# Adding halves of a group's squares on VectorE before the product of ones, and a new order in the norms

## The chip, the cores and the metric

The kernel runs on one core of one Trainium2 chip. The time is device microseconds of one execution. Most executions of this kernel agree within a few tenths of a microsecond.

## What is computed

The reference runs 512 tokens of width 1024 (with 16 meta tokens ahead in the first part) through a stack of layers in f32: differential and forgetting attention with an MLP, retention with an MLP, then a block that merges sparse attention with a state-space scan (SSD), and a last gated feed-forward. Two parts of it matter here.

Layer norm, four times (behind each mixer and each MLP), and RMS norm at other places:

```
mu = mean(x);  var = mean(square(x - mu));  y = (x - mu) * rsqrt(var + eps) * g + b
```

The gated group norm behind the scan, once for each of four groups of 512 channels:

```
u = y * silu(z);  u = u * rsqrt(mean(u * u, over the group's 512 channels) + EPS)
```

## The kernel before

Activations lie by feature: `x32` holds 8 tiles of 128 features x 528 columns (16 meta columns and 512 tokens), so a mean over features is a sum over partitions and tiles. The kernel makes it on TensorE with a stationary matrix of equal values (`ones_d`, `ones_g`). Such a product of f32 data is two matmul records of 512 columns; the 16 meta columns, in the wide norms, are two short ones more. The dense products split weights and activations in a high and a low part (f32r) and take three products for each pair.

**Weights** come through a ring of four slots (RING, AHEAD = 3). SP loads a chunk of 128x1024, ScalarE makes `w_hi` (L362), VectorE `w_lo` (L370), both three chunks ahead of the chunk that TensorE reads. SP loads a slot again when `lo_ready` says that VectorE is done with it.

Each engine has one hand-written program, and all order between engines is by semaphores. An engine that waits holds up all that stands behind in its program.

**The scan stage** (`ssm_pe`, `ssm_act`, `ssm_dve`) goes through four groups g of four chunks c each, then a fifth turn, g = 4, that only finishes the last group. Between the scan's own small products TensorE runs "items", dense chunks of other projections (`xs`, `z`, `so`, `gate`), 24 products each. The finish of group g-1 lies in the first chunk of group g:

- VectorE, at the end of group g-1, multiplies the gate in (L3161, four of 128x512), then makes group g's first chunk ready (`chunk_ready`, L3065 to L3094: dec_end, eight of seg, x_dt, b_tok, cb, x_dec, seg, c_dec), then the first item's w_lo, then `finish_norm_dve` (L3125), which waits for the root.
- ScalarE squares the four tiles into `z_buf` (L2975, `u_sq` + 1 each), does its part of chunk_ready, one w_hi, loads the logarithm's table (L1167), takes the logarithm of the mean (L1173, waits for `ssm_var`) and the exponential (L1176), which makes the inverse root.
- TensorE runs `ssm_turn`, the first item, then `squares_pe` (L2891), four products of `ones_g` with the four tiles of `z_buf`, then the next items and `ssm_outputs`.
- `so_pe` (L2876) of the group, some chunks later, multiplies the normed tiles. In the last group POOL loads `merged` back once `u_lo` is written.

**LayerNorm** (L1249) is spread over the product ahead of it. `tile_dve` (L1306) adds tile k's product to x32, sums tiles 5 and 6 into `rest` (the sum of tiles 0 to 4 made a shift, which is taken off all tiles into `xc`), and adds squares into `sq_sum` (`squares_sum`, L1334), those of tile 6 ahead of tile 7. ScalarE squares (`squares_act`). `LayerNorm.pe` (L1293) then runs filler products (`idle_products`, 18 for ln00, 12 for ln10, none for the others) and four sums: rest, sq_sum, tile 7 of x32 (the mean is whole) and the square of tile 7 (the variance is whole), and more fillers. ScalarE copies the mean (L1406), squares it (L1409), loads the logarithm's table (L1167) and makes the root of what VectorE writes at L1381 (variance less squared mean).

The callers are `even_out_dve` (L1004) for ln00 and `before_norm_dve` (L1126) for ln01, ln10 and ln11: for each chunk of the product ahead they split w_lo and call `tile_dve`. ln00 has nl = 0 and ln10 has nl = 2.

**Norm** (L1178) with `summed=True` is the RMS norm of `rms_ffn` and of `final`, the last work of the kernel: the squares of tiles 0 to 6 are summed by VectorE into `x_sum`, that of tile 7 comes from ScalarE. `final` runs ten fillers first.

Of the kernel before, what the change touches and what calls it, by code (L numbers as in the profile page):

```python
# [7 lines left out]
ALU = mybir.AluOpType  # L8
# [6 lines left out]
KT = D // P  # L15
META = 16
SEQ = 512
# [22 lines left out]
AHEAD = RING - 1  # L40
# [12 lines left out]
CHUNKS = dict(STAGES)  # L53
# [149 lines left out]
def program(nc, x_in, weights, params, tables, lam_in, w_uk, w_uv, rel, line, skewed, cum_dram, acum_dram, merged_dram, kept_dram, gate_dram, sums_dram, out):  # L203
    with ExitStack() as ctx:
# [799 lines left out]
        def even_out_dve(dve):  # L1004

            halves_before = halves_signalled(len(dense_step) - 1)
            for ck in range(4):
                split_lo(dve, Step(FIRST_CHUNK["eo_b"] + ck + AHEAD))
                for m in range(2):
                    ready = (chunk_done, FIRST_CHUNK["eo_b"] + ck + 1) if m else (half_done, halves_before + ck + 1)  # L1010
                    ln00.tile_dve(dve, "eo_b", 2 * ck + m, 1.0, ready)

        MEANS = {26: 0, 27: 1, 30: 2, 31: 3, 32: 4}

# [111 lines left out]
        def before_norm_dve(dve, name, factor, norm, outs=(), split_before=0):  # L1126

            kg = KGROUPS.get(name, 1)
            for c in range(CHUNKS[name]):
                if c >= split_before:  # L1130
                    split_lo(dve, Step(FIRST_CHUNK[name] + c + AHEAD))
                if c % kg == kg - 1:
                    norm.tile_dve(dve, name, c // kg, factor, (chunk_done, FIRST_CHUNK[name] + c + 1),
                                  out=outs[c // kg] if c // kg < len(outs) else None)

        def before_norm_act(act, name, norm, split_before=0):

# [40 lines left out]
        class Norm:  # L1178
# [28 lines left out]

            def pe(self, pe):
                if self.summed:
                    if self.last:  # L1210
                        idle_products(pe, 10, 6)
                    pe.wait_ge(sum_added, self.sums + KT - 1)
                    nc.tensor.matmul(flat[:, 3072:3072 + SEQ], ones_d[:], x_sum[:, META:T], start=True, stop=False, skip_group_check=True)
                for n, k in enumerate(self.squares):
                    pe.wait_ge(norm_squared, self.squares_before + n + 1)
                    last = nc.tensor.matmul(flat[:, 3072:3072 + SEQ], ones_d[:], self.sq[:, k, META:T],
                                            start=k == 0, stop=k == KT - 1, skip_group_check=self.summed)
                last.then_inc(norm_var, 1)
                if not self.last:
                    idle_products(pe, 22)  # L1220
# [28 lines left out]
        class LayerNorm:  # L1249
# [4 lines left out]
            def __init__(self, name, tile, wide, g, b, last=False):  # L1254
                self.sums = norms["sums"]
                norms["sums"] += KT - 2
                self.last = last
                split = norms["split"]
                norms["split"] += not last
                self.tile, self.wide, self.g, self.b = tile, wide, g, b  # L1260
                self.c0 = 0 if wide else META
                placed["next"] = norm_start
                self.xc = at(name + "_xc", [P, KT, T])
                self.sq = at(name + "_sq", [P, 3, T])
                self.sq_sum = at(name + "_sq_sum", [P, T])
                self.shift = at(name + "_shift", [P, T])
                self.rest = at(name + "_rest", [P, T])
                self.mean = at(name + "_mean", [P, T])
                self.mean_sq = at(name + "_mean_sq", [P, T])
                self.rt = at(name + "_rt", [P, T])  # L1270
                self.n, self.nl = norms["all"], norms["layer"]
                norms["all"] += 1
                norms["layer"] += 1
                self.hi_before = KT * split
                self.ready = (norm_lo, KT * split)
                self.lo_at = KT * (split + 1)
# [16 lines left out]
            def pe(self, pe):  # L1293
                idle_products(pe, {0: 18, 2: 12}.get(self.nl, 0), 6)
                pe.wait_ge(sum_added, self.sums + KT - 2)
                pe.wait_ge(ln_copied, 3 * self.nl + 1)
                self.sums_pe(2048, ones_d, self.rest, True, False)
                pe.wait_ge(ln_summed, self.summed_before() + KT - 2)
                self.sums_pe(3072, ones_d, self.sq_sum, True, False)
                tiles_out(pe, self.tile)  # L1300
                self.sums_pe(2048, ones_d, x32[:, KT - 1], False, True).then_inc(ln_means, 1)
                pe.wait_ge(ln_squared, KT * (self.nl + 1))
                self.sums_pe(3072, ones_d, self.sq[:, (KT - 1) % 3], False, True).then_inc(norm_var, 1)
                idle_products(pe, 27 if self.wide else 26)

            def tile_dve(self, dve, name, k, factor, ready, out=None):  # L1306
                u = FIRST_TILE[name] + k
                if k > SHIFT_TILES:
                    self.squares_sum(dve, {5: range(2, 4), 6: range(4, 6), 7: range(6, 7)}[k])
                dve.wait_ge(*ready)  # L1310
                o = halves(x32[:, k], self.wide)
# [18 lines left out]
                    nc.vector.tensor_tensor(self.xc[:, j, c], x32[:, j, c], self.shift[:, c], ALU.subtract).then_inc(ln_less, 1)  # L1330
                if k == SHIFT_TILES:
                    self.squares_sum(dve, range(1, 2))

            def squares_sum(self, dve, tiles):  # L1334
                c = slice(self.c0, T)
# [1550 lines left out]

        def squares_pe(pe, g):

            for t in range(4):
                pe.wait_ge(u_sq, 4 * g + t + 1)  # L2890
                last = nc.tensor.matmul(bank(1, SEQ), ones_g[:], z_buf[:, t], start=t == 0, stop=t == 3)  # L2891
            last.then_inc(ssm_var, 1)

        def ssm_pe(pe, g):
# [232 lines left out]
        def finish_lo_dve(dve, g):  # L3127
            x = xs[g % 2]
            for t in range(4):
                dve.wait_ge(u_hi_s, 4 * g + t + 1)  # L3130
                nc.vector.tensor_tensor(u_lo[:, t, META:T], x[:, t], u_hi[:, t, META:T], ALU.subtract).then_inc(u_lo_s, 1)

        waiting = []

        def ssm_dve(dve, g):

            for c, items in enumerate(group_items(g)):
                if g < SSM_GROUPS:
                    chunk_ready(dve, g, c)
                for item in waiting:  # L3140
                    item_dve(dve, item)
                waiting.clear()
                for i, item in enumerate(items):
                    item_split(dve, item, split_lo)
                    if g and c == 0 and i == 0:
                        finish_norm_dve(dve, g - 1)
                    if g and c == 0 and i == (0 if item[0] == "z" else 1):
                        finish_lo_dve(dve, g - 1)
                        item_dve(dve, items[0])
                    if not (g and c == 0 and i == 0):  # L3150
                        if item[0] == "xs" and i == len(items) - 1:
                            waiting.append(item)
                        else:
                            item_dve(dve, item)
                if g < SSM_GROUPS:
                    chunk_end(dve, g, c)
# [603 lines left out]
```

## Time and profile before

| | |
|---|---|
| median of 3 runs | 2673.89 us (2673.74 to 2673.92) |
| the profiled execution | 2673.44 us |
| its span, first to last instruction | 2671.6 us |
| TensorE matmul / weight load busy | 98% / 84% of the span |
| VectorE, ScalarE, GpSimd busy | 63%, 47%, 7% |
| mean granted TensorE clock | 0.998 |
| HBM read, written | 438 MB, 160 MB |
| chain that ended last | TensorE 85%, VectorE 8%, ScalarE 4%, issue 2%, DMA 1% |

Busy shares say which engine works, not which one is waited for. In the timelines a row is a run of instructions: start, length, engine, line, operation, tiles, count, and in brackets how long the engine was idle before it and what ended that. Rows of pipelined matmuls overlap by about 0.17 us, so a run of 512-column f32 records takes 0.43 us for each, and the last one 0.59. The windows give busy time of each engine in a stretch, the granted clock (PEclk, 1.00 is 2.4 GHz) and the DMA share.

### The profile page before, as it was taken

The page shows a single profiled execution, that of the slowest core. Times are in us where ns is not written, and L with a number is a line of the kernel's source. Part 1 is how long each engine was busy: PE and PEld are TensorE (multiplying, and loading weights), DVE is VectorE, ACT ScalarE, POOL GpSimd, SP SyncE. Part 2 cuts the span into 40 slices and gives each one's busy share as a digit, 9 for nine tenths or more (in the row PEclk, how much of TensorE's full clock was granted, in tenths as well). Part 3 has the DMA queues.
Part 4 walks back from the last instruction along what each step waited for, and adds up shares of the span by engine and source line. Part 5 has one row for each costly group of instructions (what it writes and reads, how often), then busy time and mean ns, then how long its engine had stood idle before and what let it go on. Part 6 is the DMA issues. An engine that isn't in the chain of part 4 may idle for free.

```text
span 2671.6 us, 42472 instructions
## 1 busy us (share of the span) xinstructions
PE 2617.3 (98%) x16495; PEld 2237.1 (84%) x16495; DVE 1675.3 (63%) x2902; ACT 1267.8 (47%) x2049; POOL 183.2 (7%) x234
## 2 busy tenths in 40 slices
PE   8999999999999999999999999999999999999998
PEld 7877789999998798779898786766877777799996
DVE  4544586265565465487265535875589986696784
ACT  4556465153364354356154434254464554475561
POOL 1111000000000000000000012051000000000000
PEclk9999999999999999999999999999999999999999
DMA  9994836958646564736557979922433333254451
GB/s 357 219 229 104 218 88 224 218 167 245 142 159 216 145 188 138 236 105 192 148 163 246 260 182 266 256 58 79 144 95 119 113 112 115 79 189 148 156 171 55
DMA packets 187722, 450.56 MB, mean 169 GB/s; under 512 B 14984, under 2 KB 31368, under 8 KB 186896
## 3 DMA queue, kind: packets, MB, share of 16 engines
q1 hardware_dynamic: 108368, 264.29, 29.3%
q0 software_dynamic: 60000, 167.78, 26.6%
q10 hardware_dynamic: 19168, 15.93, 2.1%
q8 instruction: 127, 2.08, 0.3%
q14 instruction: 59, 0.48, 0.1%
HBM read 438.24 MB, written 159.51 MB: 224 GB/s over the span
## 4 chain that ended last, share of the span: by engine, by line
PE 85%; DVE 8%; ACT 4%; issue 2%; DMA 1%; POOL 0%; DVEq 0%; ACTq 0%; POOLq 0%
PE ps L399 30%; PE ps L1531 25%; PE ps L549 6%; PE ps L3328 4%; PE ps L2339 2%; PE ps L1976 2%; PE ps L2130 2%; PE ps L2014 2%; PE ps L2876 2%; PE ps L791 2%; PE ps L919 1%; DVE w_lo L370 1%; ACT w_hi L362 1%; PE ps L878 1%; DVE xs L3029 1%
## 5 line engine op out<-in xcount | busy, mean ns | idle before, releaser
L370 DVE TENSOR_TENSOR w_lo<-raw,w_hi 128x1024 fp32r<-128x1024 f32 x500 | 611.0, 1222 | 472.7 <-ACT w_hi L362 471.6
L362 ACT ACTIVATE w_hi<-raw 128x1024 fp32r<-128x1024 f32 x500 | 527.0, 1055 | 517.5 <-PE ps L399 296.5
L1531 PE MATMUL ps<-x_hi,w_hi 128*128 128x264 f32 (+1 forms) x1120 | 317.4, 283 | 2.2 <-DVE rg L1910 0.7
L1531 PE MATMUL ps<-x_hi,w_lo 128*128 128x264 f32 (+1 forms) x1120 | 316.4, 282 | 0.0
L1531 PE MATMUL ps<-x_lo,w_hi 128*128 128x264 f32 (+1 forms) x1120 | 316.1, 282 | 0.0
L399 PE MATMUL ps<-x_hi,w_hi 128*128 128x512 f32 (+1 forms) x688 | 249.4, 380 | 16.1 <-DVE w_lo L370 9.4
L399 PE MATMUL ps<-x_lo,w_hi 128*128 128x512 f32 (+1 forms) x688 | 245.2, 374 | 0.0
L399 PE MATMUL ps<-x_hi,w_lo 128*128 128x512 f32 (+1 forms) x688 | 244.0, 372 | 0.0
L1531 PEld LDWEIGHTS ps<-x_hi,w_hi 128*128 128x128 f32 x1120 | 210.8, 188 | 5.1 <-issue 2.2
L1531 PEld LDWEIGHTS ps<-x_hi,w_lo 128*128 128x128 f32 x1120 | 211.1, 188 | 0.0
L1531 PEld LDWEIGHTS ps<-x_lo,w_hi 128*128 128x128 f32 x1120 | 210.6, 188 | 0.4
L399 PE MATMUL ps<-h_hi,w_hi 128*128 128x264 f32 (+1 forms) x768 | 205.8, 322 | 0.0
L399 PE MATMUL ps<-h_lo,w_hi 128*128 128x264 f32 (+1 forms) x768 | 205.2, 322 | 0.0
L399 PE MATMUL ps<-h_hi,w_lo 128*128 128x264 f32 (+1 forms) x768 | 204.6, 320 | 0.0
L399 PEld LDWEIGHTS ps<-x_hi,w_hi 128*128 128x128 f32 x688 | 125.5, 189 | 50.9 <-issue 18.7
L399 PEld LDWEIGHTS ps<-x_hi,w_lo 128*128 128x128 f32 x688 | 125.5, 190 | 23.3
L399 PEld LDWEIGHTS ps<-x_lo,w_hi 128*128 128x128 f32 x688 | 125.4, 189 | 22.9 <-issue 1.0
L399 PEld LDWEIGHTS ps<-h_lo,w_hi 128*128 128x128 f32 x768 | 127.7, 188 | 11.6 <-issue 0.2
L399 PEld LDWEIGHTS ps<-h_hi,w_lo 128*128 128x128 f32 x768 | 127.8, 189 | 11.2
L399 PEld LDWEIGHTS ps<-h_hi,w_hi 128*128 128x128 f32 x768 | 127.1, 188 | 11.6 <-issue 0.2
L549 PE MATMUL ps<-x_hi,w_hi 128*128 128x264 f32 x352 | 112.6, 320 | 0.0
L549 PE MATMUL ps<-x_hi,w_lo 128*128 128x264 f32 x352 | 100.4, 285 | 0.0
(501 smaller groups left out, 5823.9 us busy)
## 6 DMA issues: line engine op xcount, KB each, us to landing
raw<-in_weights SPq DMA_DIRECT2D x255, 512.0 KB
raw<-weight_sums SPq DMA_DIRECT2D x280, 256.0 KB
weight_sums<-in_weights POOLq DMA_DIRECT2D x36, 1536.0 KB, 20.2
raw<-in_weights SPq DMA_DIRECT2D x210, 256.0 KB
weight_sums<-in_weights POOLq DMA_DIRECT2D x12, 2048.0 KB, 31.3
weight_sums<-in_weights POOLq DMA_DIRECT2D x12, 1792.0 KB, 22.1
weight_sums<-weight_sums POOLq DMA_DIRECT2D x12, 1536.0 KB, 14.7
weight_sums<-weight_sums POOLq DMA_DIRECT2D x4, 2048.0 KB, 21.1
```

Of the source, the lines that this page charges most:

```text
L362: nc.scalar.activation(w_hi[:, s], raw[:, s], ACT.Copy).then_inc(hi_ready, 1)
L370: nc.vector.tensor_tensor(w_lo[:, s], raw[:, s], w_hi[:, s], ALU.subtract).then_inc(lo_ready, 1)
L399: last = nc.tensor.matmul(o[:, h, :], w[:, s, k], a[:, k0 + k, cols], start=start and k == 0 and n == 0, stop=stop and k == nk - 1 and n == 2)
L549: last = nc.tensor.matmul(ps[:, 2 + h, 0:HALF], a[:, g % RING, w], b[:, k, cols], start=k == 0 and n == 0, stop=half_end and n == 2)
L791: last = nc.tensor.matmul(flat[0:n, o + a:o + b], qk[rows, qt, c:c + n], qk[rows, kt_, a:b], start=True, stop=True)
L1531: last = nc.tensor.matmul(out_, w[:, s, 4 * (b % 2) + k], a, start=kind in "125" and k == n == 0, stop=k == 3 and n == 2, skip_group_check ...
L1976: last = nc.tensor.matmul(flat[:, o + SEQ - w:o + SEQ], rv[0:n, b, e * P:(e + 1) * P], decayed[0:n, b, SEQ - w:SEQ], start=b == 0, stop=b ...
L2014: last = nc.tensor.matmul(ps[:, 2 * (u % 2), 0:SEQ], w[:, g % RING, 2 * f + m], a[:, f], start=f == 0 and n == 0, stop=f == 3 and n == 2)
L2130: last = nc.tensor.matmul(open_out(t)[:, 0, :], w[:, g % RING, k], a[:, k % 4], start=k == 0 and n == 0, stop=k == KT - 1 and n == 2)
L2339: last = nc.tensor.matmul(kept_out_at(n)[:, 0, :], w[:, ck % RING, k], a[:, k, META:T], start=k == 0 and i == 0, stop=k == KT - 1 and i == 2)
L2876: last = nc.tensor.matmul(ps[:, 2 * (u % 2) + k % 2, 0:SEQ], a[:, ck % RING, 2 * f + m], b[:, f, META:T], start=f == 0 and w == 0, stop=f ...
L3328: last = nc.tensor.matmul(out_, w[:, g % RING, n], a[:, r], start=n == 0 and m == 0, stop=n == len(rows) - 1 and m == 2)
```

## The change

1. Scan: VectorE adds `z_buf[:, 2:4]` to `z_buf[:, 0:2]` (one 128x1024 f32 addition, `squares_sum_dve`), called in `ssm_dve` behind `chunk_ready` of the next group's first chunk. `squares_pe` waits for it and makes two products instead of four.
2. `LayerNorm.pe`, all four norms: the product of tile 7 moves ahead of that of `sq_sum`.
3. ln00 and ln10 (`sums_late`): the last chunk's `split_lo` and the sum of tile 6's squares move behind the work on tile 7.
4. `Norm.pe`, `final` alone: ten fillers ahead of the sums' product become five behind it, in another bank.

```diff
--- before.py
+++ after.py
@@ -1005,10 +1005,12 @@
 
             halves_before = halves_signalled(len(dense_step) - 1)
             for ck in range(4):
-                split_lo(dve, Step(FIRST_CHUNK["eo_b"] + ck + AHEAD))
+                if ck < 3:
+                    split_lo(dve, Step(FIRST_CHUNK["eo_b"] + ck + AHEAD))
                 for m in range(2):
                     ready = (chunk_done, FIRST_CHUNK["eo_b"] + ck + 1) if m else (half_done, halves_before + ck + 1)
                     ln00.tile_dve(dve, "eo_b", 2 * ck + m, 1.0, ready)
+            split_lo(dve, Step(FIRST_CHUNK["eo_b"] + 3 + AHEAD))
 
         MEANS = {26: 0, 27: 1, 30: 2, 31: 3, 32: 4}
 
@@ -1127,11 +1129,14 @@
 
             kg = KGROUPS.get(name, 1)
             for c in range(CHUNKS[name]):
-                if c >= split_before:
+                last = norm.sums_late and c == CHUNKS[name] - 1
+                if c >= split_before and not last:
                     split_lo(dve, Step(FIRST_CHUNK[name] + c + AHEAD))
                 if c % kg == kg - 1:
                     norm.tile_dve(dve, name, c // kg, factor, (chunk_done, FIRST_CHUNK[name] + c + 1),
                                   out=outs[c // kg] if c // kg < len(outs) else None)
+                if last:
+                    split_lo(dve, Step(FIRST_CHUNK[name] + c + AHEAD))
 
         def before_norm_act(act, name, norm, split_before=0):
 
@@ -1207,10 +1212,10 @@
 
             def pe(self, pe):
                 if self.summed:
-                    if self.last:
-                        idle_products(pe, 10, 6)
                     pe.wait_ge(sum_added, self.sums + KT - 1)
                     nc.tensor.matmul(flat[:, 3072:3072 + SEQ], ones_d[:], x_sum[:, META:T], start=True, stop=False, skip_group_check=True)
+                    if self.last:
+                        idle_products(pe, 5, 5)
                 for n, k in enumerate(self.squares):
                     pe.wait_ge(norm_squared, self.squares_before + n + 1)
                     last = nc.tensor.matmul(flat[:, 3072:3072 + SEQ], ones_d[:], self.sq[:, k, META:T],
@@ -1269,6 +1274,7 @@
                 self.mean_sq = at(name + "_mean_sq", [P, T])
                 self.rt = at(name + "_rt", [P, T])
                 self.n, self.nl = norms["all"], norms["layer"]
+                self.sums_late = self.nl in (0, 2)
                 norms["all"] += 1
                 norms["layer"] += 1
                 self.hi_before = KT * split
@@ -1295,17 +1301,17 @@
                 pe.wait_ge(sum_added, self.sums + KT - 2)
                 pe.wait_ge(ln_copied, 3 * self.nl + 1)
                 self.sums_pe(2048, ones_d, self.rest, True, False)
+                tiles_out(pe, self.tile)
+                self.sums_pe(2048, ones_d, x32[:, KT - 1], False, True).then_inc(ln_means, 1)
                 pe.wait_ge(ln_summed, self.summed_before() + KT - 2)
                 self.sums_pe(3072, ones_d, self.sq_sum, True, False)
-                tiles_out(pe, self.tile)
-                self.sums_pe(2048, ones_d, x32[:, KT - 1], False, True).then_inc(ln_means, 1)
                 pe.wait_ge(ln_squared, KT * (self.nl + 1))
                 self.sums_pe(3072, ones_d, self.sq[:, (KT - 1) % 3], False, True).then_inc(norm_var, 1)
                 idle_products(pe, 27 if self.wide else 26)
 
             def tile_dve(self, dve, name, k, factor, ready, out=None):
                 u = FIRST_TILE[name] + k
-                if k > SHIFT_TILES:
+                if k > SHIFT_TILES and not (k == KT - 1 and self.sums_late):
                     self.squares_sum(dve, {5: range(2, 4), 6: range(4, 6), 7: range(6, 7)}[k])
                 dve.wait_ge(*ready)
                 o = halves(x32[:, k], self.wide)
@@ -1330,6 +1336,8 @@
                     nc.vector.tensor_tensor(self.xc[:, j, c], x32[:, j, c], self.shift[:, c], ALU.subtract).then_inc(ln_less, 1)
                 if k == SHIFT_TILES:
                     self.squares_sum(dve, range(1, 2))
+                if k == KT - 1 and self.sums_late:
+                    self.squares_sum(dve, range(6, 7))
 
             def squares_sum(self, dve, tiles):
                 c = slice(self.c0, T)
@@ -2886,9 +2894,9 @@
 
         def squares_pe(pe, g):
 
-            for t in range(4):
-                pe.wait_ge(u_sq, 4 * g + t + 1)
-                last = nc.tensor.matmul(bank(1, SEQ), ones_g[:], z_buf[:, t], start=t == 0, stop=t == 3)
+            pe.wait_ge(u_sq, 5 * g + 5)
+            for t in range(2):
+                last = nc.tensor.matmul(bank(1, SEQ), ones_g[:], z_buf[:, t], start=t == 0, stop=t == 1)
             last.then_inc(ssm_var, 1)
 
         def ssm_pe(pe, g):
@@ -3130,6 +3138,11 @@
                 dve.wait_ge(u_hi_s, 4 * g + t + 1)
                 nc.vector.tensor_tensor(u_lo[:, t, META:T], x[:, t], u_hi[:, t, META:T], ALU.subtract).then_inc(u_lo_s, 1)
 
+        def squares_sum_dve(dve, g):
+
+            dve.wait_ge(u_sq, 5 * g + 4)
+            nc.vector.tensor_tensor(z_buf[:, 0:2], z_buf[:, 0:2], z_buf[:, 2:4], ALU.add).then_inc(u_sq, 1)
+
         waiting = []
 
         def ssm_dve(dve, g):
@@ -3137,6 +3150,8 @@
             for c, items in enumerate(group_items(g)):
                 if g < SSM_GROUPS:
                     chunk_ready(dve, g, c)
+                if g and c == 0:
+                    squares_sum_dve(dve, g - 1)
                 for item in waiting:
                     item_dve(dve, item)
                 waiting.clear()
```

## Rows read from the trace of the kernel before

**Rows 1.** The page, its section on busy time, share of the span, instructions.

```profile
PE 2617.3 (98%) x16495; PEld 2237.1 (84%) x16495; DVE 1675.3 (63%) x2902; ACT 1267.8 (47%) x2049; POOL 183.2 (7%) x234
```

**Rows 2.** Windows: busy time of each engine, scan stage, one group.

```profile
1993.00:2067.00 74.00, 73.76 (x403) 57.48 (x403) 67.72 (x135) 41.81 (x52) 0.80 (x1) 1.00 0.35 116
```

**Rows 3.** Waits of TensorE, whole run: total us, times, longest.

```profile
PE ps L878 <- issue: 2.3, 3, 1.8
...
PE ps L2876 <- ACT c_row L2940: 1.1, 2, 0.9
```

**Rows 4.** Timeline of TensorE: the squares' products, groups 0 to 3.

```profile
1999.24 3.60 PE L2891 MATMUL ps<-z_buf,ones_g 128*128 128x512 f32 x8
...
2072.12 3.60 PE L2891 MATMUL ps<-z_buf,ones_g 128*128 128x512 f32 x8
...
2145.70 3.60 PE L2891 MATMUL ps<-z_buf,ones_g 128*128 128x512 f32 x8
...
2212.07 3.60 PE L2891 MATMUL ps<-z_buf,ones_g 128*128 128x512 f32 x8
```

**Rows 5.** Timeline of VectorE: the w_lo behind chunk_ready, groups 1 to 3.

```profile
2003.07 1.22 DVE L370 TENSOR_TENSOR w_lo<-raw,w_hi 128x1024 fp32r<-128x1024 f32 x1
...
2076.64 1.22 DVE L370 TENSOR_TENSOR w_lo<-raw,w_hi 128x1024 fp32r<-128x1024 f32 x1
...
2150.22 1.22 DVE L370 TENSOR_TENSOR w_lo<-raw,w_hi 128x1024 fp32r<-128x1024 f32 x1
```

**Rows 6.** Timeline of ScalarE: two of the logarithms, last group's squares.

```profile
2003.90 0.67 ACT L1173 ACTIVATE z_buf<-ps,small 128x512 f32<-128x512 f32 x1
...
2077.47 0.67 ACT L1173 ACTIVATE z_buf<-ps,small 128x512 f32<-128x512 f32 x1
...
2208.39 2.44 ACT L2975 ACTIVATE z_buf<-xs 128x512 f32<-128x512 f32 x4 [3.23 <-DVE xs L3161]
```

**Rows 7.** Windows: the start, a slow stretch, the end; clock third from last.

```profile
9.00:14.40 5.40, 5.03 (x23) 5.03 (x24) 5.17 (x8) 3.54 (x7) 4.33 (x12) 1.00 0.81 273
14.40:18.00 3.60, 3.60 (x31) 3.60 (x31) 1.41 (x2) 2.10 (x3) 3.60 (x6) 1.00 1.01 383
...
151.00:154.50 3.50, 3.50 (x18) 3.15 (x18) 1.99 (x10) 1.73 (x6) 1.44 (x2) 0.51 0.26 93
...
2663.00:2671.00 8.00, 0.00 (x0) 0.00 (x0) 5.27 (x8) 0.00 (x0) 0.00 (x0) 0.51 0.69 262
```

**Rows 8.** Timelines of VectorE, ScalarE, TensorE around ln00.

```profile
345.12 1.23 DVE L370 TENSOR_TENSOR w_lo<-raw,w_hi 128x1024 fp32r<-128x1024 f32 x1 [1.66 <-ACT w_hi L362]
...
353.59 0.67 ACT L1406 ACTIVATE ln_mean<-ps 128x512 f32<-128x512 f32 x2 [0.39 <-PE ps L1285]
...
356.36 0.72 ACT L1173 ACTIVATE ln_rt<-ln_rt,small 128x528 f32<-128x528 f32 x1
...
344.64 4.18 PE L1163 MATMUL ps<-ident 128*128 128x128 f32 x36
```

**Rows 9.** Chain that ended last, at ln01: start, us, what.

```profile
719.08 3.16 PE ps L1285 x12
```

**Rows 10.** Timelines of ScalarE and TensorE at ln01, ln10, ln11.

```profile
722.26 0.67 ACT L1406 ACTIVATE ln_mean<-ps 128x512 f32<-128x512 f32 x2 [1.03 <-PE ps L1285]
...
1167.06 0.60 ACT L1406 ACTIVATE ln_mean<-ps 128x512 f32<-128x512 f32 x1
...
1164.01 1.02 PE L1285 MATMUL ps<-ln_rest,ones_d 128*128 128x512 f32 x2
...
1521.72 0.60 ACT L1406 ACTIVATE ln_mean<-ps 128x512 f32<-128x512 f32 x1 [0.50 <-PE ps L1285]
```

**Rows 11.** Timeline of all engines, the end.

```profile
2656.07 2.39 PE L1163 MATMUL ps<-ident 128*128 128x128 f32 x20
...
2658.30 1.02 PE L1213 MATMUL ps<-x_sum,ones_d 128*128 128x512 f32 x2
...
2660.22 0.69 ACT L1173 ACTIVATE final_rt<-ps,small 128x512 f32<-128x512 f32 x1 [1.08 <-PE ps L1216]
```

## The prediction

> **What bounds the kernel now.** First the page: TensorE is busy for 2617.3 of 2671.6 us [rows 1], and the waits of its engine sum to a few tens of us, so anything that stops it costs its full length. Next the scan stage by windows, one per group: from 1993 to 2067 us TensorE is busy 73.76 of 74.00 us and VectorE 67.72 [rows 2]. TensorE sets the pace and VectorE follows close behind. In that stage the waits show only 1.1 us of TensorE waiting, twice, for the activation that empties a bank into c_row [rows 3]. Last, the norms and the end, where the chain leaves TensorE: there ScalarE's copies, logarithms and table loads set the time [rows 8 to 11], and TensorE runs filler products.
>
> The sum is made against the profiled execution, 2673.44 us with a span of 2671.6; the median of the runs is 2673.89, and I add the change to that.
>
> **Scan, groups 0 to 2: the new wait.** In squares_pe the four products are 8 records of about 0.43 us pitch, 3.60 us from start to data [rows 4]. Two of the four go: 4 records, 1.72 us less. But they now wait for VectorE's addition, and in ssm_dve that stands behind chunk_ready of the next group. The first squares product starts at 1999.24 now [rows 4]; chunk_ready ends where VectorE turns to w_lo, at 2003.07 [rows 5]. The addition is 128x1024 f32, as that w_lo is, so 1.22 us: ready at 2004.33 with 0.04 for the signal. TensorE stands for 5.1 us, with all later products of the stage queued behind the wait. Its data are then there at 2004.33 + 3.60 - 1.72 = 2006.21, against 2002.84: **3.37 us late**. ScalarE's logarithm started at 2003.90, with 1.06 to spare [rows 6]; it now starts at 2006.25, and with it the scaling on VectorE, the evictions and everything VectorE does until the next group slip by 2.35. The addition's own 1.13 on VectorE lies inside that.
>
> TensorE gains back 0.24 of its 1.1 us of waiting for c_row in this group and 0.86 in the next, since it is now later than ScalarE by more than that [rows 3]. Group 1: the addition is ready at 2076.64 + 2.35 + 1.26 = 2080.25, data at 2082.13 instead of 2075.72 (2072.12 + 3.60): 6.41 late, 5.55 after the c_row wait; the logarithm moves from 2077.47 to 2082.17, 4.70 [rows 4 to 6]. Group 2: 2150.22 + 4.70 + 1.26 + 1.88 = 2158.06 against 2149.30, **8.76 late**.
>
> **Scan, group 3.** No chunk_ready stands ahead here. ScalarE's squares end at 2208.39 + 2.44 = 2210.83 [rows 6], the addition at 2212.1, the product wants them at 2212.07 [rows 4]: no wait to speak of, and 1.7 us are saved. ScalarE waits for this product, so u_lo, and the merged tile loaded behind it, come earlier with it. Scan in all: 8.8 - 1.7 = **+7.1**.
>
> **Scan, the clock.** TensorE never waits longer than 1.8 us in this trace [rows 3]. After its last product, done at 2660.2, the granted clock is at half, 1.2 GHz, from 2663 on [rows 7, 11]; it also fell once among sparse products, from 151 to 154.5 us [rows 7]. Three stops of some 5 us each are longer than those 3 us, so I take it that each of them ends in a fall. The price: a stretch of 3.4 us at 1.2 GHz costs half of it, 1.7, in products; the dense start of the run was slow for 5.4 us (23 products, against 31 in the 3.6 us behind it [rows 7]), which would be 2.6. The lower bound is 0, no fall. Near the 151 row, and since part of the slow stretch may lie in the stop itself, I take 1.6 for each: nearly all of it falls on the squares' own products, so it also delays the logarithm and is not caught up. **+4.8**.
>
> The Trainium skill, "TensorE: Matmul & The Clock Gate", section on what is actually happening, puts it as "the default state is throttled, and activity releases the throttle"; this speaks against the change, as the half clock at the end of the trace does. Without a fall the scan would be +7.1, with falls +11.9.
>
> **Norms: mean before squares, on PE.** In LayerNorm.pe the product of tile 7 now comes second, not third. One set of products is 3.16 / 3 = 1.05 us with the meta columns [rows 9] and 0.86, two records of 0.43, without [rows 4]. The mean's copy on ScalarE is the head of its chain: copy, square, table, logarithm. ln01: ScalarE waited 1.03 for it, so it gains 1.0; the variance then comes last, at 719.08 + 4.2, leaving **0.9** [rows 9, 10]. ln11: ScalarE waited 0.50 [rows 10]: **0.5**. ln10: TensorE's first sums start behind the fillers at 1164.01 [rows 10], the mean is there at 1164.01 + 1.72 + 0.15 = 1165.9 instead of 1167.06: **1.2**; the sum of squares moved behind tile 7 must be ready by then and, with w_lo gone from ahead of it, is.
>
> ln00 has most. VectorE was late there: TensorE was done with its tiles at 344.64 and ran fillers to 348.82 [rows 8]. The w_lo and its 1.66 of waiting leave the chain, 2.8 us, and the last sum of squares 0.6 more. So the four sets of products start at 348.82, straight behind the fillers, which now decide: mean at 348.82 + 2.1 + 0.15 = 351.1 instead of 353.59, variance at 353.2, root's input (two operations, 0.8) at 354.05 against the logarithm's 356.36 [rows 8]: **2.3**. The moved w_lo costs nothing: it runs while VectorE waits for ScalarE (1.8 us now), and its weights are wanted some chunks later; without that cover it would cost its 1.14 twice. Its slot's next load on SP is issued about 4 us later, and the ring of four slots has it wanted only four chunks on.
>
> **The end.** The ten fillers run from 2656.07 for 2.2 us, the sums' product starts at 2658.30, the last square's after it [rows 11]. Now the sums' product goes first, then five fillers, and the square's comes five fillers sooner, 1.1 us. ScalarE had waited 1.08 for it and can follow: **1.0**.
>
> Norms and end: 2.3 + 0.9 + 1.2 + 0.5 + 1.0 = 5.9, so **-5.9**. All: 7.1 + 4.8 - 5.9 = **+6.0**, 2679.9 us.
>
> **The rivals.**
> - **The clock holds** (or falls once): +7.1 - 5.9 = +1.2, 2675.1; with one fall 2676.7. For it: the 1.8 us wait left it full, and the scan around the stops is dense. Against it: the fall 3 us after the last product. 0.24.
> - **The norms give little:** the orders move a wait from one engine to the next (the root's input, gated by the variance, takes the mean's place in ln00 and ln01). With half of the 5.9, 2682.8. Against it: each gain stands in ScalarE's own idle time. 0.12.
> - **Longer slow stretches,** 2.6 each in place of 1.6, and VectorE then waits for TensorE at the end of each group: 2683 to 2684. 0.08.
> - **The other side, faster:** the addition is ready when TensorE wants it. Then four groups save 1.72 each, 6.9, and with the norms 12.8: 2661.1. It takes chunk_ready ending 5 us sooner in the queue; the point is 1998.0 for its end in group 0. The rows have it at 2003.07, 2076.64 and 2150.22 against 1999.24, 2072.12 and 2145.70 [rows 4, 5], each time 4 to 5 us late. 0.06.
>
> **How the numbers follow.** My forecast has 0.5. A measurement of this kernel tells some 0.2%, 5.3 us, from no change; the edge is 2679.2, just below my time, so of the 0.5 I count 0.15 as the same (two falls, or slightly larger norms) and 0.35 as slower. Slower: 0.35 + 0.12 + 0.08 = 0.55. Same: 0.15 + 0.24 = 0.39. Faster 0.06. The range leaves out the fast rival and the top of the long-stretch one, and gives the smallest case 1 us below for the norms: 2674.1 to 2683.8.
>
> **What would show it.** TensorE waiting on VectorE's z_buf, three times, 4.5 to 5.2 us each, and not in the last group; granted clock below full in the windows around 2005, 2082 and 2160. The logarithm of the groups 2.4, 4.7 and 7 us later against its group's start of now, plus the clock's share. ScalarE's mean copy of ln00 near 351.1, its logarithm near 354.1; the last logarithm 1.0 sooner after the last fd2 product. I am wrong if TensorE's wait at the squares is under 2 us, or if the stretch up to 1990 us, where only norms changed, is not about 4.9 us shorter.

## The result and the profile after

The changed kernel takes **2683.03 us** (2680.25 to 2685.14, 7 runs) against 2673.74 (2672.36 to 2673.92, 7 runs) for the one before, a ratio of 1.0031 with an interval of 1.0022 to 1.0040: slower by more than the 0.2% that can be told. The forecast was 2679.9, in a range up to 2683.8. The profiled execution took 2681.20 us (span 2679.4), 7.8 more than that of before. All that follows is read in it.

The page, busy times, against [rows 1]:

```profile
PE 2614.9 (98%) x16469; PEld 2235.2 (83%) x16469; DVE 1680.4 (63%) x2906; ACT 1268.7 (47%) x2049; POOL 183.2 (7%) x234
```

TensorE is busy for 2.4 us less, and the kernel is longer. The waits of TensorE, whole run (engine, line, waited for: us in total, times, longest), against [rows 3]:

```profile
PE ps L2899 <- DVE z_buf L3144: 14.9, 3, 5.0
...
PE ps L878 <- issue: 2.3, 3, 1.8
```

A wait that did not exist now heads the list, 14.9 us in three waits of 5 us. (The list, of before too, also has one wait of over 9 us for a w_lo of VectorE, L399; it lies ahead of the kernel's first product.) L2899 is the product of ones, L3144 the new addition. Where it stands, in the timeline of TensorE, against [rows 4]:

```profile
1999.35 3.78 PE L2899 MATMUL ps<-z_buf,ones_g 128*128 128x512 f32 x4 [4.95 <-DVE z_buf L3144]
2077.28 3.78 PE L2899 MATMUL ps<-z_buf,ones_g 128*128 128x512 f32 x4 [4.95 <-DVE z_buf L3144]
2155.51 3.78 PE L2899 MATMUL ps<-z_buf,ones_g 128*128 128x512 f32 x4 [4.96 <-DVE z_buf L3144]
2222.52 1.98 PE L2899 MATMUL ps<-z_buf,ones_g 128*128 128x512 f32 x4
```

Three stops in brackets, none in the last group. The same four records take 3.78 us behind a stop and 1.98 in the last group: these two numbers are the two clocks. VectorE and ScalarE around the first stop, against [rows 5, 6] (their timelines):

```profile
1996.95 1.22 DVE L3102 TENSOR_TENSOR c_dec<-steps_abc,c_row 128x1024 f32<-128x1024 f32 x1
1998.08 1.22 DVE L3144 TENSOR_TENSOR z_buf<-z_buf 128x1024 f32<-128x1024 f32 x1
...
2003.17 0.69 ACT L1178 ACTIVATE z_buf<-ps,small 128x512 f32<-128x512 f32 x1 [4.18 <-PE ps L2899]
...
2081.09 0.69 ACT L1178 ACTIVATE z_buf<-ps,small 128x512 f32<-128x512 f32 x1 [4.17 <-PE ps L2899]
...
2159.33 0.69 ACT L1178 ACTIVATE z_buf<-ps,small 128x512 f32<-128x512 f32 x1 [4.17 <-PE ps L2899]
...
2224.54 0.69 ACT L1178 ACTIVATE z_buf<-ps,small 128x512 f32<-128x512 f32 x1 [0.87 <-PE ps L2899]
```

The addition starts where `chunk_ready` ends, with c_dec. ScalarE, which had 1 us to spare at its logarithm, now waits 4.2 us for TensorE. The clock, in windows (columns as in [rows 2]):

```profile
1985.00:1996.00 11.00, 9.41 (x68) 7.40 (x66) 8.71 (x25) 9.09 (x11) 0.00 (x0) 1.00 0.44 132
1996.00:2004.00 8.00, 4.65 (x8) 2.42 (x9) 4.44 (x4) 3.77 (x6) 0.00 (x0) 0.57 0.24 81
2004.00:2012.00 8.00, 8.00 (x36) 6.48 (x35) 6.16 (x9) 6.75 (x10) 0.80 (x1) 1.00 0.09 11
2075.00:2082.50 7.50, 5.22 (x9) 2.85 (x10) 3.35 (x3) 3.28 (x5) 0.00 (x0) 0.54 0.21 71
2153.00:2161.00 8.00, 5.49 (x10) 3.03 (x11) 3.59 (x4) 3.78 (x5) 0.00 (x0) 0.57 0.22 76
```

A PEclk of 0.57 over 8.00 us is 2 x 0.43 x 8.00 = 6.9 us at 1.2 GHz, around each of the three stops. The clock's own record begins at 1996.7, some 2.3 us into the stop, and lasts 6.8; in the other two stops the fall comes 2.9 and 3.2 us in.

The norms gained. ln00 on ScalarE, against [rows 8], and the end on TensorE and ScalarE, against [rows 11]:

```profile
350.83 0.67 ACT L1414 ACTIVATE ln_mean<-ps 128x512 f32<-128x512 f32 x2 [1.84 <-PE ps L1291]
...
353.80 0.74 ACT L1178 ACTIVATE ln_rt<-ln_rt,small 128x528 f32<-128x528 f32 x1
...
2664.90 1.02 PE L1216 MATMUL ps<-x_sum,ones_d 128*128 128x512 f32 x2
2665.76 1.28 PE L1168 MATMUL ps<-ident 128*128 128x128 f32 x10
2666.87 1.02 PE L1221 MATMUL ps<-final_sq,ones_d 128*128 128x512 f32 x2
2667.93 0.69 ACT L1178 ACTIVATE final_rt<-ps,small 128x512 f32<-128x512 f32 x1
```

**Where the time went.** One point to read from: E, the end of the first group's `chunk_ready` (2003.07 before, 1998.08 after, where the next VectorE row starts). It came 4.99 earlier. From E to the four logarithms:

| us behind E | group 0 | 1 | 2 | last |
|---|---|---|---|---|
| before | 0.83 | 74.40 | 147.98 | 212.63 |
| after | 5.09 | 83.01 | 161.25 | 226.46 |
| later by | 4.26 | 8.61 | 13.27 | 13.83 |

And from the last to the final logarithm the end saves 1.12: 13.83 - 4.99 - 1.12 = 7.7, which is the difference between the two final logarithms, 2660.22 and 2667.93. Only the split of 13.83 into stop and clock is not to be read from this trace.

### The profile page after: what moved, and what is told of

Its sections match the earlier page's. It is cut to its first block, busy times and chain, and to the rows that moved or that the text cites. A ratio compares the mean times of both kernels' runs of the same rounds, so it can differ in the third digit from the quotient of the medians.

```text
span 2679.4 us, 42424 instructions
## 1 busy us (share of the span) xinstructions
PE 2614.9 (98%) x16469; PEld 2235.2 (83%) x16469; DVE 1680.4 (63%) x2906; ACT 1268.7 (47%) x2049; POOL 183.2 (7%) x234
## 4 chain that ended last, share of the span: by engine, by line
PE 86%; DVE 7%; ACT 4%; issue 2%; DMA 1%; POOL 0%; DVEq 0%; ACTq 0%; POOLq 0%
PE ps L399 31%; PE ps L1539 25%; PE ps L549 6%; PE ps L3343 4%; PE ps L2347 2%; PE ps L1984 2%; PE ps L2138 2%; PE ps L2022 2%; PE ps L791 2%; PE ps L919 1%; PE ps L2884 1%; DVE w_lo L370 1%; PE ps L878 1%; ACT w_hi L362 1%; PE ps L982 1%
## 5 line engine op out<-in xcount | busy, mean ns | idle before, releaser
L399 PE MATMUL ps<-x_hi,w_hi 128*128 128x512 f32 (+1 forms) x688 | 251.2, 382 | 14.1 <-DVE w_lo L370 9.7
L399 PE MATMUL ps<-x_lo,w_hi 128*128 128x512 f32 (+1 forms) x688 | 245.6, 374 | 0.0
L399 PE MATMUL ps<-x_hi,w_lo 128*128 128x512 f32 (+1 forms) x688 | 244.2, 372 | 0.0
L399 PE MATMUL ps<-h_hi,w_hi 128*128 128x264 f32 (+1 forms) x768 | 205.9, 322 | 0.0
L399 PE MATMUL ps<-h_lo,w_hi 128*128 128x264 f32 (+1 forms) x768 | 205.2, 322 | 0.0
L399 PE MATMUL ps<-h_hi,w_lo 128*128 128x264 f32 (+1 forms) x768 | 204.8, 321 | 0.0
L399 PEld LDWEIGHTS ps<-x_hi,w_hi 128*128 128x128 f32 x688 | 126.0, 190 | 49.7 <-issue 17.2
L399 PEld LDWEIGHTS ps<-x_lo,w_hi 128*128 128x128 f32 x688 | 125.7, 190 | 23.8 <-issue 1.8
L399 PEld LDWEIGHTS ps<-x_hi,w_lo 128*128 128x128 f32 x688 | 125.7, 190 | 23.5
L399 PEld LDWEIGHTS ps<-h_lo,w_hi 128*128 128x128 f32 x768 | 127.9, 188 | 11.8 <-issue 0.2
L399 PEld LDWEIGHTS ps<-h_hi,w_lo 128*128 128x128 f32 x768 | 127.8, 188 | 11.2
L399 PEld LDWEIGHTS ps<-h_hi,w_hi 128*128 128x128 f32 x768 | 127.1, 188 | 11.7 <-issue 0.2
```

What stands on the lines that cost most here:

```text
L399: last = nc.tensor.matmul(o[:, h, :], w[:, s, k], a[:, k0 + k, cols], start=start and k == 0 and n == 0, stop=stop and k == nk - 1 and n == 2)
```

## The experiments

All ratios are to the kernel before, run beside them. `idle_products(pe, n, b)` makes n 128x128 fillers.

**Parts of the change, each alone.** The change with its scan part undone (four products again, no addition):

```diff
-            pe.wait_ge(u_sq, 5 * g + 5)
-            for t in range(2):
+            for t in range(4):
+                pe.wait_ge(u_sq, 4 * g + t + 1)
...
-                if g and c == 0:
-                    squares_sum_dve(dve, g - 1)
```

> The change without its scan part: four products of ones, no addition. Theory (the scan's stops and the slow clock cost more than the norms give): the norms and the end give what their logarithms show in the trace of after, 4.99 us up to the scan and 1.1 at the end, so 2673.7 - 6.1 = 2667.6 us, with no stop of TensorE in the scan and the clock of before. Rival (the norms' gains are partly an effect of where the scan part put things, or are lost again at later waits): 2670 us or more.

Measured: 2667.47 us (11 runs), 0.9978 (0.9969 to 0.9987). Its profiled execution is 5.97 below that of before.

The scan part alone, on the kernel before (the reverse of these lines, and no other):

> The kernel before with the scan part alone. Theory: 2683.0 + 6.1 = 2689.1 us; three stops of 5.0 us before the squares' products, each with 6.8 us of half clock. Rival (the two parts are not additive: the half clock comes from where the shortened norms put the stops): under 2686.

Measured: 2688.02 us (5 runs), 1.0053 (1.0040 to 1.0067), with the same three stops of 4.95 us. But the first of them has less of the half clock, in its timeline and window:

```profile
2005.36 0.90 PE L2891 MATMUL ps<-z_buf,ones_g 128*128 128x512 f32 x1 [4.95 <-DVE z_buf L3136]
```

```profile
2000.00:2008.00 8.00, 3.05 (x7) 1.21 (x5) 6.33 (x9) 4.96 (x7) 0.00 (x0) 0.86 0.23 65
```

Here the clock falls 0.4 us behind the stop and stays at half for 3.4 us, where 6.8 were expected; the other two stops have 6.8 each. The same stop does not always bring the same fall. From its E, 2004.08, the last logarithm is 226.02 away, after's 226.46. The parts hardly touch each other: 2667.47 + 2688.02 - 2673.40 = 2682.1, and the whole measured 2683.0.

**Is it the place of the wait, or the addition?** Norms, four products, nothing added; they only wait for `chunk_ready`:

```diff
+            if g < SSM_GROUPS - 1:
+                pe.wait_ge(y_ready, CH * (g + 1) + 1)
             for t in range(4):
```

> Norms as changed, scan as before with four products and no addition, but in groups 0 to 2 TensorE waits ahead of them for the end of chunk_ready on VectorE. Theory (the place of the wait costs, not the addition): stops of 3.8 us, four products at half clock in place of two, logarithms some 4.8 us later per group, in all 2673.7 + 16 - 6 = 2683.7 us. Rival (the 1.2 us of addition on an almost full VectorE is the cost): about 2668 to 2672.

Measured: 2683.56 us (5 runs), 1.0040 (1.0026 to 1.0053). Its waits and timeline of TensorE:

```profile
PE ps L2901 <- DVE c_dec L3104: 11.8, 3, 4.0
```

```profile
1998.95 2.87 PE L2901 MATMUL ps<-z_buf,ones_g 128*128 128x512 f32 x3 [3.80 <-DVE c_dec L3104]
```

About as slow as the change, without its addition: a wait for `chunk_ready` in that place is enough, whatever VectorE computes behind it. The two totals are not made of the same parts. These stops are 3.8 to 4.0 us, not 4.95 (the rest is the addition), four products stand behind each in place of two, and the half clock lasts 3.4 us, not 6.8.

**How much of it is the clock?** The change with fillers where TensorE stops, so that it is busy until the addition is there, nothing else moved:

```diff
+            if g < SSM_GROUPS - 1:
+                idle_products(pe, 21, 7)
             pe.wait_ge(u_sq, 5 * g + 5)
```

> The changed kernel with 21 filler products on TensorE ahead of its wait for the sum, in groups 0 to 2. The wait for VectorE stays as long, only the engine is not idle in it. Theory (each stop costs the wait and, by the clock's fall, nearly 2 us more): no half clock in the scan, the squares' four records 1.9 us in place of 3.8, scan 7.1 in place of 13.8, in all about 2673.7 + 7.1 - 6.1 = 2674.7 us. Rival (the fall costs little, the rest of the scan's loss is in VectorE's longer work and what waits for it): 2681 or more.

Measured: 2678.31 us, 1.0013 (1.0004 to 1.0022), but the 11 executions have two times: five took 2673.6 to 2675.1, six 2678.3 to 2679.2. The profiled one took 2673.61. Its timelines of TensorE and ScalarE:

```profile
1993.39 4.85 PE L1168 MATMUL ps<-ident 128*128 128x128 f32 x42
1998.49 1.98 PE L2901 MATMUL ps<-z_buf,ones_g 128*128 128x512 f32 x4 [0.26 <-DVE z_buf L3146]
...
2000.52 0.69 ACT L1178 ACTIVATE z_buf<-ps,small 128x512 f32<-128x512 f32 x1 [2.38 <-PE ps L2901]
```

and its windows, where the clock stays whole:

```profile
1996.00:2010.00 14.00, 13.74 (x67) 10.79 (x66) 10.28 (x14) 9.67 (x14) 0.80 (x1) 1.00 0.26 66
```

The products are held as long (1998.49 is 1.27 us behind E, 1999.35 in the change too) and take 1.98 us in place of 3.78. From its E (1997.22) the logarithms stand at 3.30, 79.35, 155.42 and 219.99: later than before by 2.47, 4.95, 7.44 and 7.36. That is the stop without the clock. The rest of 13.83, **6.5 us, is the clock's**.

The kernel with fillers has a second group of times, near 2678.6. One guess was that short fillers do not always hold the clock, so 512-column ones were put in their place:

```diff
+            if g < SSM_GROUPS - 1:
+                for _ in range(5):
+                    nc.tensor.matmul(bank(7, SEQ), ident[:], x32[:, 0, META:T], start=True, stop=True, skip_group_check=True)
+                idle_products(pe, 2, 7)
```

> The changed kernel with the stop filled by five products of 512 f32 columns and two short ones in place of 21 short ones (those left the clock at 0.998 in 5 of 11 executions, some 2674, and at 0.996 in 6, some 2678.6). Theory (the difference is three falls of 1.6 us each, and denser products hold the clock): all executions near 2674, none at 2678. Rival (the two times have another cause): both times again.

Measured: 2675.44 us (11 runs), 1.0007 (0.9998 to 1.0016): seven executions 2673.8 to 2676.1, three 2678.7 to 2678.9, one 2682.2. Its logarithms stand at 3.29, 79.34, 155.41 and 219.96 behind E, the other fillers' to 0.03. So the longer times do not come from the kind of filler. The kernel before has them too: beside this run 4 of its 15 executions took 2677.5 to 2678.0. A candidate comes with the next kernel's trace.

**What are two products less worth, if they cost nothing?** Norms, two of the four products, no addition and no new wait (the squares of tiles 2 and 3 are left out of the group's mean):

```diff
-            pe.wait_ge(u_sq, 5 * g + 5)
             for t in range(2):
+                pe.wait_ge(u_sq, 4 * g + t + 1)
```

> Norms as changed; in the scan TensorE makes two of the four products and nothing is added: the squares of tiles 2 and 3 are left out of the group norm. This is the most that any cheaper sum could bring. Theory (in groups 0 to 2 the chain through ScalarE and VectorE sets the pace once TensorE is 1.7 us shorter: c_row, conv_in and z_buf empty the banks no sooner): TensorE waits at the evictions for nearly what it saves, and only the last group's 1.7 us and at most 1 us of the rest come through: 2667.5 - 2.3 = 2665.2 us. Rival (TensorE sets the pace, as its 99% in the scan's windows says): 2667.5 - 6.9 = 2660.6.

Measured: 2666.09 us (5 runs), 0.9966 (0.9952 to 0.9979), 1.4 below norms alone, where the saving in four groups would be 6.9 and the theory had 2.3. By medians the 1.4 is hardly clear of the scatter; the trace is clearer. Its logarithms of groups 0 to 2 stand at 2003.11, 2076.68 and 2150.27: a group takes 73.57 us, as before, and only the last group's logarithm is nearer to E, by 1.72 (210.92 against norms alone's 212.64). Its waits of TensorE, most of them not in the list before:

```profile
PE ps L399 <- ACT z_buf L2953: 1.7, 1, 1.7
PE ps L2884 <- ACT c_row L2948: 1.7, 2, 0.9
PE ps L399 <- ACT conv_in L2940: 1.6, 2, 1.1
```

In groups 0 to 2 the 1.7 us become waits for ScalarE; only the last group keeps them. The idea had next to no headroom there, whatever it cost.

Its profiled execution (2669.71, the longest of its five) also has this window; the second row is that of the kernel before:

```profile
221.00:232.00 11.00, 11.00 (x32) 6.15 (x31) 1.11 (x5) 5.85 (x15) 1.88 (x2) 0.53 0.28 51
```

```profile
221.00:232.00 11.00, 11.00 (x58) 7.07 (x56) 2.87 (x14) 8.46 (x21) 1.88 (x2) 1.00 0.25 44
```

At 0.53, 10.3 us at half clock, 32 products in place of 58, behind a wait of 1.8 us (L878) that leaves the clock full in 12 of the 14 traces. The code is the same there in all kernels. It costs 4.05 us: the last product ahead of ln00 starts at 348.62, in norms alone at 344.57. That this makes the longer times of the two filler kernels and of before is likely by its size, but not shown: their long executions have no trace.

**Other places for the addition.** Ahead of `chunk_ready` on VectorE:

```diff
+                if g and c == 0:
+                    squares_sum_dve(dve, g - 1)
                 if g < SSM_GROUPS:
                     chunk_ready(dve, g, c)
```

> The changed kernel with VectorE's addition ahead of chunk_ready in place of behind it. Theory (VectorE follows TensorE so closely that what delays it comes back): no stop at the squares, but VectorE stands 0.7 us for ScalarE's last square and adds for 1.2, so chunk_ready and the logarithm come 2.0 later in groups 0 to 2, and TensorE waits for it at c_row's bank; 2667.5 + 3 * 2.0 - 1.7 = 2671.8 us, clock full. Rival (VectorE has the slack, the wait at the squares was all): 2660.6.

Measured: 2672.93 us (11 runs), 0.9995 (0.9985 to 1.0004): 5.5 slower than norms alone. Its waits of TensorE and VectorE:

```profile
PE ps L399 <- ACT conv_in L2940: 3.9, 2, 1.9
PE ps L399 <- ACT z_buf L2953: 2.5, 1, 2.5
```

```profile
DVE z_buf L3144 <- ACT z_buf L2983: 2.8, 4, 0.7
```

The stop is gone, but VectorE waits 0.7 for the squares and adds for 1.13, four times, with everything behind it; TensorE meets that as waits of 1.9 to 2.5, and after each the trace shows 3.4 us at half clock, where the theory had it full. A group takes 75.3 us in place of 73.6. In 3 of the 11 executions the mean clock was 0.998 or more, and these took 2669.8 to 2670.7: even with the clock held the place costs some 3 us.

On GpSimd, two additions of 128x512, which nothing else seemed to want:

```diff
+        def squares_sum_pool(pool, g):
+            for t in (0, 2):
+                pool.wait_ge(u_sq, 4 * g + t + 2)
+                nc.gpsimd.tensor_tensor(z_buf[:, t], z_buf[:, t], z_buf[:, t + 1], ALU.add).then_inc(head_var, 1)
```

> Norms as changed; the group's squares are added in pairs on GpSimd (two additions of 128x512), the first as soon as two squares are there, and TensorE makes two products. Theory (the sum itself is sound, only its place behind chunk_ready costs): GpSimd is idle here; with some 1.4 us for each addition, estimated as twice the 0.68 us of its 128x256 additions, the sums are there when TensorE wants them, no stop, 1.7 us saved in each of four groups: 2667.5 - 6.9 = 2660.6 us. Rival (GpSimd slower than that on two f32 operands while VectorE is busy, or VectorE the real bound of the stage, so that a shorter TensorE only waits elsewhere): 2664 to 2668.

Measured: 2672.03 us (11 runs), 0.9993 (0.9984 to 1.0002): no better, and above the rival's 2664 to 2668 too. GpSimd and VectorE at the first group, in their timelines:

```profile
1991.86 2.78 POOL L2766 TENSOR_TENSOR z_buf<-z_buf 128x512 f32<-128x512 f32 x2 [98.40 <-ACT z_buf L2991]
...
1992.16 1.26 DVE L3091 TENSOR_TENSOR dec_end<-steps_abc,acum_tok 128x8 f32<-128x8 f32 x1
1993.35 2.74 DVE L3095 TENSOR_SCALAR seg<-steps_abc,acum_tok 128x128 f32<-128x128 f32 x8
```

The same two rows of VectorE in the kernel before:

```profile
1997.36 0.16 DVE L3075 TENSOR_TENSOR dec_end<-steps_abc,acum_tok 128x8 f32<-128x8 f32 x1
1997.44 1.65 DVE L3079 TENSOR_SCALAR seg<-steps_abc,acum_tok 128x128 f32<-128x128 f32 x8
```

While GpSimd adds, one small operation of VectorE for each addition takes 1.1 us longer: dec_end, and the first of the eight of seg (1.37 us; the other seven take 0.27 each, as before). These 2.2 us are more than the addition that VectorE was to be spared. TensorE meets them as waits of 2.3 to 3.0 us, and again 3.4 us at half clock follow each. A group takes 75.4 us. The five executions at a mean clock of 0.998 took 2670.4 to 2671.3, so here too most of the loss remains without the fall.

**Parts of the norms.** The new order on TensorE alone, on the kernel before, and then the late sums, late w_lo and the end with the old order:

```diff
+                tiles_out(pe, self.tile)
+                self.sums_pe(2048, ones_d, x32[:, KT - 1], False, True).then_inc(ln_means, 1)
                 pe.wait_ge(ln_summed, self.summed_before() + KT - 2)
                 self.sums_pe(3072, ones_d, self.sq_sum, True, False)
-                tiles_out(pe, self.tile)
-                self.sums_pe(2048, ones_d, x32[:, KT - 1], False, True).then_inc(ln_means, 1)
```

> The kernel before with only the order of the products in LayerNorm.pe changed. Theory: 0.9 in ln01 and 0.6 in ln11, 0.6 in ln00 where VectorE is still late, nearly 0 in ln10 where ScalarE's last square ends with the mean: 2.1 us, 2671.4. Rival (the order alone brings the whole of the norms' 5 us): 2668.5.

> The kernel before with the late sum of squares and w_lo in ln00 and ln10 and the new fillers at the end, but the old order of the four products. Theory: ln00 1.5, ln10 nearly 0, the end 1.1: 2.6 us, 2670.9; so the two halves are not additive with the 2.1 of the other order alone, together they give 6. Rival (additive): 6.0 - 2.1 = 3.9 us, 2669.6.

Measured: 2672.67 us, 0.9998 (0.9989 to 1.0007), and 2670.62 us, 0.9990 (0.9981 to 0.9999), 11 runs each. By medians the order alone brings 1.0 us (expected 2.1, and within its scatter), the rest alone 3.0 (expected 2.6), both together 6.0. The traces tell more, read from the last product ahead of ln00, since the profiled execution of the order alone came there 0.87 us late, with 6.8 us at half clock near 149 us where before has 3.4. From there the order alone brings 1.99 up to E, as expected: 0.27 in ln00, 0.96 in ln01, 0.16 in ln10 and 0.61 in ln11. The rest alone brings 3.02: 1.58 in ln00, 0.25 in ln10, 1.00 at the end and 0.19 between. So the parts sum to 5.0 of the 6.0, and what they add by being together lies where both act: ln00 gains 2.47 in norms alone and ln10 1.07. There the late sums get VectorE out of the way, and then the mean can be first.

**Fewer fillers in ln00.** With the work on VectorE moved, the 18 fillers decide when the sums start. Norms alone with 8:

```diff
-                idle_products(pe, {0: 18, 2: 12}.get(self.nl, 0), 6)
+                idle_products(pe, {0: 8, 2: 12}.get(self.nl, 0), 6)
```

> norms_only with 8 fillers in place of 18 ahead of ln00's sums. Theory (with VectorE's work reordered the fillers decide there): sums start at 346.4 in place of 348.6, the variance then waits for tile 7's square, logarithm 1.7 us sooner: 2665.8 us. Rival (the 10 fillers kept the clock up through the norm): a half clock near 350 us and 2668 or more.

Measured: **2665.51 us** (2664.34 to 2666.28, 5 runs), 0.9963 (0.9950 to 0.9977): 8.2 below the kernel before and 17.5 below the change. Its timeline of ScalarE:

```profile
349.31 0.67 ACT L1414 ACTIVATE ln_mean<-ps 128x512 f32<-128x512 f32 x2
...
352.56 0.73 ACT L1178 ACTIVATE ln_rt<-ln_rt,small 128x528 f32<-128x528 f32 x1 [0.38 <-DVE ln_rt L1389]
```

ScalarE no longer waits for the mean, and the logarithm waits for VectorE. It is 1.24 us earlier than after's, and 1.64 against the last product ahead of ln00, which came 0.40 later in this execution; 1.7 were expected. The granted clock is 1.00 near 350 us, so the rival, which needs the fillers for the clock, fails.

**The addition where it is in time.** That kernel, with the addition and the two products in the last group only:

```diff
+            last_group = g == SSM_GROUPS - 1
-            for t in range(4):
-                pe.wait_ge(u_sq, 4 * g + t + 1)
+            for t in range(2 if last_group else 4):
+                pe.wait_ge(u_sq, 4 * g + (5 if last_group else t + 1))
```

> norms_fewer_fillers, and the addition with two products in the last group alone, where no chunk_ready stands ahead of it. Theory: no stop, 1.7 us on the path: 2665.8 - 1.7 = 2664.1 us, faster than both kernels. Rival (merged's load or ScalarE decides there, not the products): 2665.8.

Measured: 2665.53 us (2663.09 to 2668.52, 5 runs), 0.9961 (0.9948 to 0.9975). In its timelines the products and the logarithm of the last group:

```profile
2209.81 1.98 PE L2900 MATMUL ps<-z_buf,ones_g 128*128 128x512 f32 x4
...
2211.83 0.69 ACT L1178 ACTIVATE z_buf<-ps,small 128x512 f32<-128x512 f32 x1 [0.87 <-PE ps L2900]
```

From the first group's logarithm (2001.57) to this one are 210.26 us; without the addition they are 211.78 (1997.23 to 2209.01). So 1.5 us are gained in this place, and 1.44 are left between E and the final logarithm (654.51 against 655.95): the products did decide there, against the rival. The medians show none of it. The profiled execution has the stretch at 221 us as well, which put its last product ahead of ln00 at 348.70, 3.87 us later than in the version above. Whether this version is the better one by its run times stays open.

## Why the prediction was right, and what it mis-sized

- **The stop: right.** 5.1 us forecast, 4.95 measured, three times, and none in the last group. Without the clock the four logarithms were to be 2.35, 4.70, 7.05 and 7.1 later; the kernel with fillers has 2.47, 4.95, 7.44 and 7.36. The reason given, that VectorE's queue has `chunk_ready` ahead of the addition, is shown by the waiting kernel: a wait for `chunk_ready` alone makes stops of 3.8 to 4.0 us, and the addition the rest.
- **What the two products save: right in the sum, wrong in the fast rival.** The prediction took 1.72 off each delay, and behind a stop that holds, since there ScalarE waits for these products. The fast rival, at 0.06, took the same 1.72 as a gain in four groups, 6.9 in all. The kernel with two products shows that groups 0 to 2 could not have kept it: there TensorE only waits longer for ScalarE, and an addition in time would have left the last group's 1.5 to 1.7.
- **The clock: right in kind, the mis-sized term.** "I take 1.6 for each", +4.8 in all, from the 3.4 us stretch of [rows 7]; it measured 6.5, 2.2 for each. The stretches were twice as long, 6.8 us, and partly lay in the stop. The four records of the squares alone took 1.80 more; from group to group the loss was 1.79, 1.87 and 2.17, and 0.64 more by the last logarithm. The longer-stretch rival had 2.6 each, so the price came out between the two. Two readings behind the term were loose. The 2.6 came from the slow products of the start, but these rows have a PEclk of 1.00 [rows 7], so they give no price of the clock. And "TensorE never waits longer than 1.8 us" holds only behind the first product; ahead of it stands a wait of 9.4. Half clock begins within these stops, so the Trainium skill's "the default state is throttled, and activity releases the throttle" ("TensorE: Matmul & The Clock Gate", What's actually happening) agrees with the trace: the windows show 0.54 to 0.57 around the stops, and 1.00 with fillers in them. The rival in which the clock holds is refuted.
- **The norms: right.** Logarithm by logarithm, each less what came in with it: ln00 2.47 (forecast 2.3; the logarithm is 2.56 earlier, 0.09 of it from ahead of the norm), ln01 0.88 (0.9), ln10 1.09 (1.2), ln11 0.61 (0.5; its first sums came 0.33 late by what lies between ln10 and it), the end 1.12 (1.0). At the scan 4.99 of the 4.9 expected were there, and norms alone are 6.0 shorter for 5.9. The fillers were named as what decides ln00 next; with ten fewer the logarithm came 1.64 earlier.
- **The sum:** 13.83 - 4.99 - 1.12 = +7.7 in the profiled executions for +6.0, the difference being the clock (+1.7). The median is at +9.3; the runs of the changed kernel spread over 4.9 us, and the profiled one is among the short ones. What makes the others longer has no trace.

## What to carry to other kernels

An operation moved to a less busy engine is priced by its place in that engine's queue: here 1.2 us of addition stood behind 4 us of work, and the bounding engine waited for all of it. First ask what the saved work is worth if it were free; leaving it out in one kernel tells, and here three groups of four gave nothing. And if TensorE has to stand for some microseconds anyway, products for nothing in the gap can keep its clock, as they did here: nearly half of this change's cost in the scan (6.5 of 13.8 us) was not the wait but the slow products behind it.

## What the runs showed of the hardware

- At TensorE stops of 4.95 us the clock was at half for 6.8 us in five of six (the change, and its scan part alone), beginning 2.3 to 3.2 us into the stop; in the sixth for 3.4 us, beginning 0.4 us behind it. Stops of 3.8 and 4.0 us were followed by 3.4 us at half. So were waits of 1.9 to 2.5 us (addition ahead of `chunk_ready`) and 2.3 to 3.0 us (addition on GpSimd). A wait of 1.8 us near 219 us, the same in every kernel, left the clock full in 12 of 14 traces; in two it was followed by 10.2 us at half, with TensorE busy all through them. The length of a wait alone does not tell, and neither does being busy afterwards.
- GpSimd's f32 additions (1.4 us each) held up VectorE, even an operation of eight columns: 0.16 became 1.26 us, and of eight of 0.27 each the first became 1.37. The Trainium skill ("SBUF — State Buffer", Who interferes with whom) has a VectorE instruction with two SBUF inputs contend with a GpSimd one that reads SBUF, the later one waiting until the first is done; the two rows agree for dec_end, which ends with the first addition (1993.42 and 1993.40). An idle GpSimd is no free place for f32 sums beside a busy VectorE.
- Executions of one kernel differ by where the clock falls: a stretch at half clock near 150 us is 3.4 us long in some traces and 6.8 in others, with the same code, and the longer one puts what follows some 0.9 us later. Differences of 1 to 2 us between single profiles here are to be read from a common point such as E, not from the start of the run.
